# Last value loads in freed rooms, new keys last in the sum, and the gate half of the output projection drawn into the attention's last slots

## What is computed

```
for layer in range(DEPTH):
    h = rms_norm(x, g_mix[layer])
    q, k, v, ... = split(h @ w_in)
    ...
    if layer % 2 == 0:   # forgetting attention (softmax), beside a spatial gating unit
    else:                # stick-breaking attention, beside a gated short convolution
    y = concatenate([attention (512 wide), gate branch (512 wide)]) @ w_out
    x = x + y
    h = rms_norm(x, g_mlp[layer])
    x = x + square(relu(h @ w_up)) @ w_down
```

## Time and profile before

| | us |
|---|---|
| median of 3 runs | 1629.09 |
| lowest and highest | 1628.17, 1631.01 |
| the profiled execution | 1626.17 |
| its span, first to last instruction | 1624.5 |
| TensorE busy | 1520.4 |
| VectorE busy | 730.4 |
| ScalarE busy | 518.5 |
| attention stage of L0, about 196 to 356 us of the span | 160 |
| attention stage of L1, about 899 to 1147 us of the span | 248 |

### The profile page before, as it was taken

One profiled execution on the slowest core, in us unless ns is written; L12 is line 12 of the kernel. 1 busy time (PEld: TensorE's weight loads), 2 busy tenths in 40 slices (PEclk: granted clock), 3 DMA queues, 4 the chain that ended last, 5 costly groups with the idle time before them and its releaser, 6 DMA issues.

```text
span 1624.5 us, 30903 instructions
## 1 busy us (share of the span) xinstructions
PE 1520.4 (94%) x12030; PEld 1412.5 (87%) x12030; DVE 730.4 (45%) x1200; ACT 518.5 (32%) x776; POOL 65.2 (4%) x123
## 2 busy tenths in 40 slices
PE   7999988879999999999999889887899999999997
PEld 6998855559999999999999776664899999999996
DVE  5544554435444343343543564555454433434344
ACT  4211233323333131231321366465233312213122
POOL 4400000000000000000000110000000000000000
PEclk9999999989999999999999999898899999999998
DMA  6421557742232223222342437563222232322322
GB/s 172 109 69 50 182 173 226 217 136 66 78 90 82 87 77 90 78 85 84 91 145 75 157 117 215 173 190 114 70 78 83 85 91 78 90 78 77 91 78 72
DMA packets 241143, 178.74 MB, mean 110 GB/s; under 512 B 9940, under 2 KB 205080, under 8 KB 241050
## 3 DMA queue, kind: packets, MB, share of 16 engines
q1 hardware_dynamic: 237514, 172.29, 36.1%
q0 software_dynamic: 3536, 5.20, 1.0%
HBM read 170.20 MB, written 7.26 MB: 109 GB/s over the span
## 4 chain that ended last, share of the span: by engine, by line
PE 85%; DVE 5%; ACT 4%; issue 2%; SPq 2%; DMA 2%; POOL 0%; DVEq 0%; ACTq 0%
PE BP L1547 64%; PE BU L1848 3%; PE BP L1556 3%; PE BK L1722 2%; PE BD L1831 2%; PE BD L1803 2%; PE BD L1547 1%; PE BP L1760 1%; SPq L436 1%; DMA VR<-in_cache_fox_v_dram 1%; ACT PP L724 1%; SPq L437 1%; PE BP L1773 1%; ACT KTB L717 1%; PE BD L1638 0%
## 5 line engine op out<-in xcount | busy, mean ns | idle before, releaser
L603 ACT ACTIVATE WH<-WR 128x1024 fp32r<-128x1024 f32 x165 | 173.6, 1052 | 372.7 <-PE BP L1547 368.8
L922 DVE TENSOR_TENSOR WL<-WR,WH 128x1024 fp32r<-128x1024 f32 x188 | 230.1, 1225 | 43.2 <-ACT WH L593 21.3
L1547 PE MATMUL BP<-HH,WH 128*128 128x288 f32 x1120 | 239.8, 296 | 0.5 <-DVE WL L922 0.5
L1547 PE MATMUL BP<-HH,WL 128*128 128x288 f32 x1120 | 238.8, 295 | 0.0
L1547 PE MATMUL BP<-HL,WH 128*128 128x288 f32 x1120 | 238.7, 295 | 0.0
L1547 PE MATMUL BP<-H2H,WH 128*128 128x288 f32 x1024 | 218.8, 295 | 1.2 <-DVE WL L922 1.2
L1547 PE MATMUL BP<-H2L,WH 128*128 128x288 f32 x1024 | 218.8, 294 | 0.0
L1547 PE MATMUL BP<-H2H,WL 128*128 128x288 f32 x1024 | 217.2, 293 | 0.0
L949 DVE TENSOR_TENSOR X<-BP,X 128x288 f32 (+1 forms) x156 | 64.1, 453 | 264.7 <-PE BP L1547 243.4
L1547 PEld LDWEIGHTS BP<-HH,WH 128*128 128x128 f32 x1120 | 179.7, 188 | 1.1 <-DVE WL L922 0.7
L1547 PEld LDWEIGHTS BP<-HH,WL 128*128 128x128 f32 x1120 | 179.8, 188 | 0.0
(11 more groups left out here) (351 smaller groups left out, 2016.1 us busy)
## 6 DMA issues: line engine op xcount, KB each, us to landing
WR<-in_w_up_dram SPq DMA_DIRECT2D x64, 512.0 KB, 4.0
WR<-in_w_down_dram SPq DMA_DIRECT2D x64, 512.0 KB, 3.6
KR<-in_cache_fox_k_dram SPq DMA_DIRECT2D x64, 256.0 KB, 2.9
VR<-in_cache_fox_v_dram SPq DMA_DIRECT2D x64, 256.0 KB, 2.9
VR<-in_cache_sb_v_dram SPq DMA_DIRECT2D x64, 256.0 KB, 3.3
KR<-in_cache_sb_k_dram SPq DMA_DIRECT2D x64, 256.0 KB, 2.8
WR<-in_w_in_odd_dram SPq DMA_DIRECT2D x24, 512.0 KB, 4.0
WR<-in_w_in_even_dram SPq DMA_DIRECT2D x20, 512.0 KB, 4.0
```

The costliest lines, as they stand in the source:

```text
L603: A(WH[1 - u][:], WR[1 - u][:], ACT.Copy).then_inc(S["w_high"], 1)
L922: V.tensor_tensor(WL[u][:], WR[u][:], WH[u][:].bitcast(F32), ALU.subtract).then_inc(S["w_low"], 1)
L1547: last = M(B[b + h][:, 0:TH], w[w0][:, k, :], x[:, k, h * TH:(h + 1) * TH], start=(k == 0 and n == 0), stop=(k == KT - 1 and n == 2))
```

## The change

1. **Room of the last pair's values.** For p = 3 the group g = 2 is loaded into KR (the room of key pages), once the layer's last page has been turned, and g = 3 into the first half of VR, once g = 0 has been used. They have semaphores of their own (`v_last0`, `v_last1`). SP issues g = 2 in its slot 16 (ahead of g = 1, which stands in slot 17) and g = 3 in slot 18, before in 18 and 19.
2. **New keys last.** In every pair of both layers the matmuls of the new keys and the wait for PTN move from the start of g = 0 to the end of g = 3.
3. **Gate chunks of the output projection.** The 24 matmuls of unit u = 0 on the gate branch (`side_part(0)`) go to the end of slot 18, ahead of `weighted_values(3)`; those of u = 1 (`side_part(1)`) go behind slot 19. The 48 matmuls of the attention chunks follow after `os_low`.
4. **L1 halves spread evenly.** Three units per four slots: one half in slots 4c and 4c+2, two in slots 4c+1 and 4c+3, none in 16 and 17. `conv(c)` is in slot 4c+2 on DVE. The cuts of weights go to slots 4c, 4c+1 and 4c+3, the split of the gate branch to slot 17, and the cuts for `G_OUT[1] + 1` to slot 18.

The rest of the diff writes the slot loop out as a list for each engine; in L0 it leaves the order on ACT and DVE as it was.

```diff
+        def v_tile(p, g, jj):
+            if p == NPAIR - 1 and g >= 2:
+                return KR[:, jj, :] if g == 2 else VR[:, jj, :]
             return VR[:, 4 * (g % 2) + jj, :]
+        def v_ready(L, p, g):
+            if p == NPAIR - 1 and g >= 2:
+                return f"v_last{g - 2}", 64 * (L + 1)
+            return f"v_in{L}_{g % 2}", 64 * (2 * p + g // 2 + 1)
...
-        def first_slot(L, j):
-            return j if j < 6 else 2 * j - 6
+        def first_slot(j):
+            return 4 * (j // 3) + (0, 1, 3)[j % 3]
...
-        SIDE_OUT = [{1: (0, 1), 2: (2, 3)}, {18: (0, 1, 2, 3)}]
+        SIDE_OUT = [{1: (0, 1), 2: (2, 3)}, {17: (0, 1, 2, 3)}]
...
-                    if t >= 2:
+                    if p == NPAIR - 1 and g >= 2:
+                        if g == 2:
+                            sp.wait_ge(S["k_turned"], NB * PG * (L + 1))
+                        else:
+                            sp.wait_ge(S["v_used"], t - 2)
+                    elif t >= 2:
                         sp.wait_ge(S["v_used"], t - 1)
...
-                            if (p > 0 or g > 1) and s == 4 * p + 4 + g:
+                            if (p > 0 or g > 1) and s == 4 * p + 4 + (g if p < NPAIR - 1 or g < 2 else 0 if g == 2 else 2):
                                 load_v(p, g)
...
                     if g == 0:
                         pe.wait_ge(S["pts_act"], NPAIR * L + p + 1)
                         pe.wait_ge(S["pts_dve"], NPAIR * L + p + 1)
-                        pe.wait_ge(S["ptn_set"], NPAIR * L + p + 1)
-                        for c in range(CT):
-                            M(B5[32 * c:32 * c + 32, 0:P], PTN[:, c, :, :], VN[0:NS, TT, c * P:(c + 1) * P], start=True, stop=False)
...
+                    if g == 3:
+                        pe.wait_ge(S["ptn_set"], NPAIR * L + p + 1)
+                        for c in range(CT):
+                            last = M(B5[32 * c:32 * c + 32, 0:P], PTN[:, c, :, :], VN[0:NS, TT, c * P:(c + 1) * P], start=False, stop=True)
                     last.then_inc(S["v_used"], 1)
...
+                def side_part(u):
+                    pe.wait_ge(S["w_low"], G_OUT[L] + 3 + u)
+                    pe.wait_ge(S["side_low"], CT * (L + 1))
+                    pe.wait_ge(S["pt_act"], NTASK * L + NTASK - 1 + u)
+                    pe.wait_ge(S["pt_second"], NTASK * L + NTASK - 1 + u)
+                    for k in range(CT, KT):
+                        unit_chunk(u, k, k == CT, False)
...
+                    if k == 18:
+                        side_part(0)
+                side_part(1)
+
+                pe.wait_ge(S["os_low"], L + 1)
+                for k in range(CT):
+                    pe.wait_ge(S["o_low"], CT * L + k + 1)
+                    for u in range(2):
+                        last = unit_chunk(u, k, False, k == CT - 1)
```

More of the change, by code:

```diff
@@ L1550, in unit, with unit_chunk @@
                 return body
+            def unit_chunk(u, k, first, final):
+                for n, (w, x) in enumerate(((WH, HH), (WH, HL), (WL, HH))):
+                    for h in range(2):
+                        last = M(B[2 * u + h][:, 0:TH], w[u][:, k, :], x[:, k, h * TH:(h + 1) * TH],
+                                 start=(first and n == 0), stop=(final and n == 2))
+                return last
             def pair_chunk(k, m):
                 for u in range(2):
-                    for n, (w, x) in enumerate(((WH, HH), (WH, HL), (WL, HH))):
-                        for h in range(2):
-                            last = M(B[2 * u + h][:, 0:TH], w[u][:, k, :], x[:, k, h * TH:(h + 1) * TH],
-                                     start=(m == 0 and n == 0), stop=(m == KT - 1 and n == 2))
+                    last = unit_chunk(u, k, m == 0, m == KT - 1)
                     if m == KT - 1:
                         last.then_inc(S["unit_done"], 1)
-            def first_pair(g, order, wait):
-                pe.wait_ge(S["w_low"], g + 4)
-                pe.wait_ge(S["evac_dve"], g + 2)
-                for m, k in enumerate(order):
-                    wait(k)
-                    pair_chunk(k, m)
             def rms(z):
@@ L1820, in sample_values @@
                 def sample_values(p, g):
[L1821 removed]
+                    name, count = v_ready(L, p, g)
+                    pe.wait_ge(S[name], count)
                     if g == 0:
@@ L1830, in sample_values @@
                         for c in range(CT):
-                            last = M(B5[32 * c:32 * c + 32, 0:P], PTS[:, 4 * (g % 2) + jj, c, s:s + 2, :], v_tile(g, jj)[:, c * P:(c + 1) * P],
-                                     start=False, stop=(g == 3 and jj == 3))
+                            last = M(B5[32 * c:32 * c + 32, 0:P], PTS[:, 4 * (g % 2) + jj, c, s:s + 2, :], v_tile(p, g, jj)[:, c * P:(c + 1) * P],
+                                     start=(g == 0 and jj == 0), stop=False)
+                    if g == 3:
+                        pe.wait_ge(S["ptn_set"], NPAIR * L + p + 1)
+                        for c in range(CT):
+                            last = M(B5[32 * c:32 * c + 32, 0:P], PTN[:, c, :, :], VN[0:NS, TT, c * P:(c + 1) * P], start=False, stop=True)
                     last.then_inc(S["v_used"], 1)
@@ L1892, in _ @@
                             fox_rows()
-                    if p >= 0 and o == 1:
-                        sample_values(p, 0)
-                    if p >= 0 and o == 3:
-                        turn_rows(p)
-                    if L == 1 and k == 18:
+                    if L == 1 and k == 17:
                         pe.wait_ge(S["tail_set"], 1)
@@ L1902, in _ @@
                         last.then_inc(S["tail_turned"], 1)
-                def attention_out(k):
-                    if k >= CT:
-                        pe.wait_ge(S["side_low"], CT * L + k - CT + 1)
-                    else:
-                        pe.wait_ge(S["o_low"], CT * L + k + 1)
-                    if k == 0:
-                        pe.wait_ge(S["os_low"], L + 1)
-                first_pair(G_OUT[L], [*range(CT, KT), *range(CT)], attention_out)
+                    if k == 18:
[6 more added lines that the diff above has]
+                        last = unit_chunk(u, k, False, k == CT - 1)
+                        if k == CT - 1:
+                            last.then_inc(S["unit_done"], 1)
                 pe.wait_ge(S["w_low"], G_OUT[L] + 5)
```

531 lines of the change are left out of this document (360 added, 171 removed).

## The result

The changed kernel takes 1614.03 us (median of 4 runs, 1609.72 to 1615.6), the kernel before 1630.05 (4 runs, 1628.17 to 1633.37). The ratio is 0.9888, with a 95% interval of 0.987 to 0.9906: 16.0 us faster by the medians, 18.3 by the ratio. The forecast was 1611.0, within 1604.5 to 1619.0. Its direction and size held; by the medians the sum was 2 us too hopeful. The profiled execution took 1609.72 us, 16.45 less than that of before.

The account below looks back on a forecast made before the run. It took TensorE's idle time (29 and 42 us) and the low clock in the two attention stages as what can be won; -6.5 - 0.6 - 14.7 + 3.6 = -18.2 us gave 1611 us, range 1604.5 to 1619.

Parts of the forecast that it names:

- slots 0 and 1: L1: slots 0, 2 and 4 each lose one half, -2.2 us each less 0.2 for a copy; -2.0 here.
- slots 9 and 13: L1: each gains one half and takes on slot 5's content; +1.3 us for the two, between +0.5 and +3.3.
- the other slots: L1: the slots behind 5 and 9 begin warmer or without a wait for a half; -1.0 us.
- (a): L1 end: slots 16 and 17 lose a half each, new keys go behind, a convolution wait goes; -4.8 us together.
- (b) to (e): L1 end: value waits -5.3, wait for the cut -4.2, gate split in slot 17 +0.9, clock in the pair -1.3 us.
- slack of 3 us: End of L0: TensorE reaches the fourth group 10.1 us after the first group's end; its load needed 7.1.
- the two waits go because of the rooms: End of L0: with the loads early, the waits for values of 1.62 and 3.11 us go, 4.7 us.
- New keys in L0: L0's other three pairs: first group need not wait for the last small copy, 0.2 us each; -0.6, bounds 0 and -2.
- the two signs of being wrong: L1: a half waits long for BU, or ScalarE's extra cut in the second slots comes to set `turn_sample`.
- Rival 2: L1 slots 5, 9, 13: VectorE's scans collide with two GpSimd products each; +7.0 us on the forecast, 1618; chance 0.17.
- Rival 1: L1 groups cost more than the ends give: 9.1 us a group, 1638; decides from 7.0 us a group; chance 0.07.
- Rival 4: Both layers' ends: loads come late all the same, waits of 4.7 and 5.3 us stay; -8.2 us, 1621; chance 0.05.
- rival 3: More idle time filled: slots 9 and 13 free, body at 0, full clock at both ends; -23.3 us, 1606; chance 0.15.

Follow-up runs that it names:

- again: The changed kernel itself timed again, as yardstick for the undo kernels: median 1608.91 us, ratio 0.9881 to the kernel before.
- undo_side: Changed kernel with the gate chunks of both units behind slot 19 again, ahead of the attention chunks: 1610.86 us, ratio 0.9894 to the kernel before.
- undo_rooms: Changed kernel with the last pair's third and fourth group of values back in VR, as before: 1618.08 us, ratio 0.9932 to the kernel before.
- fixed_rows: Changed kernel with L0's pages of values read from fixed places, no page numbers read for them: 1598.77 us, ratio 0.9808 to the kernel before.
- values_by_gpsimd: last_half_17 with L0's value loads, except the last pair's third and fourth group, issued by GpSimd instead of SyncE: 1599.47 us, ratio 0.9819 to the kernel before.
- weights_first: Changed kernel with ScalarE's sample_weights ahead of the cut of weights in L1 slots 5, 9 and 13: 1607.49 us, ratio 0.9857 to the kernel before.
- last_half_17: weights_first with the last unit's second half moved from slot 15 to slot 17 of L1: 1605.62 us, ratio 0.9848 to the kernel before.
- halves_16_17: last_half_17 with the last unit's first half also moved, from slot 15 to slot 16: 1601.35 us, ratio 0.9829 to the kernel before.
- small_products: Changed kernel with GpSimd's first two products of each group on 8 of 576 columns: 1613.27 us, ratio 0.9898 to the kernel before.

## Why the prediction was right

The time lies within the forecast's own range (1607 to 1615). The terms at the ends hold to about 1 us, those between less well. The last two columns are two profiles of the same program, both against the profile of before:

| term | forecast | changed | again |
|---|---|---|---|
| L0, first group of p = 3 to the end of the pair | -6.5 | -7.4 | -6.3 |
| L0 before that, counted from its first page | -0.6 | +0.7 | -3.9 |
| L1, slots 0 and 1 | -2.0 | +0.4 | +0.4 |
| L1, slots 2 and 4 | -4.0 | -3.6 | -3.6 |
| L1, slots 7, 11, 15 | +8.3 | +8.4 | +8.4 |
| L1, slot 3 | +1.0 | +1.1 | +1.1 |
| L1, slots 9 and 13 | +1.3 | +2.0 | +2.2 |
| L1, the other slots | -1.0 | -2.9 | -2.7 |
| L1, (a) slots 16 and 17 to the first group | -4.8 | -3.7 | -3.7 |
| L1, (b) to (e) | -9.9 | -10.8 | -10.8 |
| sum | -18.2 | -15.9 | -19.0 |

The rest to the 16.45 us is outside the stages' parts (0.5 at the start of L0). The sum is closer than its terms: what slots 0 and 1, (a) and slots 9 and 13 gave too little (2.4, 1.1 and 0.7 us), the other slots and (b) to (e) gave too much (1.9 and 0.9). And since L0 differs by 3.5 us between the two profiles, a match within 2 us says no more than that. That much of it is luck.

- **The ends.** Both waits for values and the wait for WL went, the fourth group follows the third, and `side_part(1)` covers `os_low` but for 0.1 us. The slack of 3 us that I gave the fourth group's load was less: without the 3.4 us of `side_part(0)` ahead of it the fourth group waits 0.87 us in L0 and 1.7 in L1 (undo_side), so it is 2.5 and 1.7 us. The clock came back in part: the pair's 96 matmuls took 13.1 us in L0 (3.38 + 9.70) and 13.5 in L1 (3.42 + 3.42 + 6.66), where I wanted 12.7 at the best and had 13.73 and 14.38 before. But undo_rooms shows that the step "the two waits go because of the rooms" credits one part with what two do: without the rooms, the moved chunks cover most of it.
- **New keys in L0, the step that failed.** I priced them at 0.2 us a pair, with the bounds "0 (the loads of values set the pace)" and -2. TensorE gained far more at first: at the end of the second group of p = 2 the changed kernel stood at 309.63 us, before at 314.62. Then came the fourth group (first the changed kernel, then before):

```profile
320.20 1.93 PE L1921 MATMUL BD<-VR,PTS 128*32 128x128 f32 x32 [2.84 <-DMA VR<-in_cache_fox_v_dram]
```

```profile
323.12 1.08 PE L1831 MATMUL BD<-VR,PTS 128*32 128x128 f32 x32 [0.77 <-DMA VR<-in_cache_fox_v_dram]
```

  Its wait is 2.84 us, not 0.77, with a low clock behind it, and by the first group of p = 3 (339.14 against 338.94) all of it was given back. In `again` the waits for values are 2.9 us, not 6.2, and counted from L0's first page the first group of p = 3 comes 3.9 us earlier than before. So the term came out at +0.7 and at -3.9, on either side of both bounds. SyncE's issue paces that stage (fixed_rows, values_by_gpsimd). I had named the loads as a bound and never costed SyncE's queue, though the chain of the earlier trace rows shows its loads standing one behind the other.
- **Slots 0 and 1, a term mis-sized.** I took slot 4 against slot 8 for the value of a half, 2.2 us, and applied it to slot 0. Slots 0 and 1 took 25.4 us against 25.05: the granted clock was 0.80 there and 1.00 before. undo_side has the same program in these slots and took 21.6 us there at a granted clock of 1.00, with the same idle time (4.5 us, 4.3 in the changed kernel): the work that left was worth 3.4 us, and the lower clock took all of it back in most executions. Why the clock falls in most and not in all is open; I read it as the work of the half that is gone from between two waits, which I have not tested.
- **Slots 9 and 13.** 36.0 us together where I had 35.2; ScalarE's cut is about 0.9 of the wait in each (weights_first). That is one of the two signs of being wrong that I had named; it came, and was too small to move the time out of the range.
- **(a)** was sized by the idle time that the halves had filled; the wait for PP behind them grew from 1.66 to 4.4 us, at a clock of 0.68. Taking two halves (6.3 us of work at 3.17 each) and the rest of (a) out of slots 16 and 17 gave 3.7 us, and last_half_17 and halves_16_17 get 2.7 and 1.2 us back by leaving them there.
- **Rival 2.** Its mechanism came in full (three slots with 3.73 us of scans), its price did not: 0, not 7. I had written against it that ScalarE's chain might hide it, and that is what it does.
- **Rival 1.** The groups from slot 5 and slot 9 took 54.6 us each, against 52.3 and 51.5: 2 to 3 more, not 7. **Rival 4** did not occur, **rival 3** neither.

## What to carry to other kernels

When a change takes waits away in a stage, ask of every queue that feeds it how full it is, the one that only issues loads too: eight loads at 1.09 us are a floor of 8.7 us for a slot, whatever TensorE does, and a gain above it comes back as a wait further on. A half unit moved out of a place with idle time cost its full length where it went (3.5 and 4.0 us in slots 7 and 11) and gave less where it was (1.4 and 2.2 in slots 4 and 2, none in slots 0 and 1 as long as the clock fell); so keep filler work in the waits and move only what someone waits for. Two engines that collide cost something only if the one that stands still is waited for: read the wait behind it before pricing it.

## What was not expected of the hardware

- SyncE needs 1.09 us to issue one load whose page it reads from a table, about 0.5 us when the address is fixed (four in 1.85 us, fixed_rows). GpSimd needs 1.13 to 1.16 for the first kind (values_by_gpsimd).
- The clock after one and the same wait (2.85 us for Pd in slots 5 and 9) came back at different times: 0.91 over slot 5 in the changed kernel, 0.82 in small_products and, with the changed kernel's own program in L1, in fixed_rows; 18.0, 19.4 and 19.1 us long. With 1.91 us of wait it stayed at 1.00 in slot 9 of weights_first and the slot took 15.7, but in its slots 5 and 13 it was 0.90, behind the same wait, and they took 17.3.
- The L0 stage of one program took 167.9 to 174.7 us in different executions while SyncE's queue was full; in the two kernels in which it was not, the stage took 155.9 and 159.2 us. The runs of one of these two agreed within 2.6 us, those of the other within 11.6, so a full queue alone does not explain the spread.
